# A two-stack fp32 model on one core: one norm's rows left unscaled between the stacks, and the first block's order of work rebuilt

## The reference, cut to what is computed

```python
def rmsnorm(x, g):
    return x * rsqrt(mean(x * x, -1) + EPS) * g

def short_conv_pool_mixer(h, w_in, conv_w, pool_w, pool_scale, w_out):   # first block
    u, gate_c, gate_b, pv = split(h @ w_in)                # 4 x 512 columns
    z = causal_conv3(gate_c * u, conv_w)
    y_a = gate_b * z
    pooled = [running_mean(pv_g, w) - pv_g for g, w in (2, 4, 8, 16)]
    y_b = (pooled @ pool_w) * pool_scale
    return concat(y_a, y_b) @ w_out

# first stack
mem_n = rmsnorm(mem, mem_norm)
h = x
h = h + short_conv_pool_mixer(rmsnorm(h, mix_norm[0]), ...)
h = h + memory_cross_attn(rmsnorm(h, xattn_norm[0]), mem_n, ...)
h = h + peer_ffn(rmsnorm(h, peer_norm[0]), ...)
# second layer: sparse attention + HGRN mixer, cross attention, peer_ffn
h = rmsnorm(h, final_norm)
# second stack, first layer: MLA + dilated attention
hn = rmsnorm(h, attn_norm_2[0])
c_q, c_kv, k_r, qB, kB, vB = split(hn @ e_w_in_2)
qA = rmsnorm(c_q, g_q) @ w_uq                              # ... attention, output projection
h = h + mix                                                # h is the normed one
# swiglu, sliding-window attention, swiglu, rmsnorm
```

## Time and profile before

| | |
|---|---|
| median of 3 runs | 2925.32 us (2921.53 to 2931.91) |
| profiled execution | 2916.09 us |
| its span | 2914.3 us |
| mean granted clock of PE | 0.983 of 2.4 GHz |
| busy: PE / DVE / ACT / POOL | 2777.4 / 1997.9 / 1467.2 / 357.9 us |
| DMA | 546.19 MB, 187 GB/s over the span |

### The profile page before, as it was taken

How to read it: one execution, slowest core, us unless ns; L and a number is a source line. 1 busy time by engine, 2 the same in 40 slices (tenths; PEclk the granted TensorE clock), 3 DMA queues, 4 the chain that set the end, 5 groups by cost and what they waited for, 6 DMA issues and landing times.

```text
span 2914.3 us, 57278 instructions
## 1 busy us (share of the span) xinstructions
PE 2777.4 (95%) x19576; PEld 2604.7 (89%) x19576; DVE 1997.9 (69%) x4331; ACT 1467.2 (50%) x2412; POOL 357.9 (12%) x207
## 2 busy tenths in 40 slices
PE   6899899999999999989999999999999799999998
PEld 6889799999988888878898999988888689999998
DVE  5556964887467667686598788557677676666665
ACT  4445345444455555455544444445555565455544
POOL 0003785000000000000179100000000000000000
PEclk8999999999999999899999999999999899999999
DMA  4434466545676665324355554666666434553454
GB/s 157 174 145 174 163 213 214 178 172 179 223 258 239 240 245 194 136 96 159 117 198 195 184 178 173 202 238 243 236 247 237 160 112 153 183 201 144 174 188 174
DMA packets 140451, 546.19 MB, mean 187 GB/s; under 512 B 15784, under 2 KB 81592, under 8 KB 83616
## 3 DMA queue, kind: packets, MB, share of 16 engines
q1 hardware_dynamic: 63216, 455.38, 43.5%
q10 hardware_dynamic: 73728, 67.14, 7.4%
q0 software_dynamic: 3376, 21.88, 1.9%
HBM read 505.53 MB, written 40.91 MB: 188 GB/s over the span
## 4 chain that ended last, share of the span: by engine, by line
PE 71%; DVE 10%; DMA 7%; POOL 5%; ACT 4%; issue 3%; SPq 0%; ACTq 0%; DVEq 0%
PE bank L779 21%; PE bank L781 20%; PE bank L780 20%; DMA ring<-in_w_stream 6%; POOL wL L542 5%; PE bank L997 4%; DVE wL L542 3%; ACT wH L532 3%; PE bank L900 1%; PE bank L920 1%; PE bank L911 1%; PE bank L796 1%; PE bank L1110 1%; DVE sq L1763 0%; DVE act_out L1750 0%
## 5 line engine op out<-in xcount | busy, mean ns | idle before, releaser
L542 DVE TENSOR_TENSOR wL<-ring,wH 128x1024 fp32r<-128x1024 f32 x742 | 906.3, 1224 | 651.5 <-ACT wH L532 647.6
L532 ACT ACTIVATE wH<-ring 128x1024 fp32r<-128x1024 f32 x864 | 908.2, 1055 | 411.9 <-DMA ring<-in_w_stream 211.6
L779 PE MATMUL bank<-hnH,wH 128*128 128x256 f32 x3528 | 1019.5, 289 | 38.2 <-DVE wL L542 18.1
L780 PE MATMUL bank<-hnL,wH 128*128 128x256 f32 x3528 | 1001.8, 284 | 0.0
L781 PE MATMUL bank<-hnH,wL 128*128 128x256 f32 x3528 | 1001.7, 284 | 0.0
L779 PEld LDWEIGHTS bank<-hnH,wH 128*128 128x128 f32 x3528 | 680.0, 193 | 47.7 <-issue 17.3
L780 PEld LDWEIGHTS bank<-hnL,wH 128*128 128x128 f32 x3528 | 680.6, 193 | 0.8 <-issue 0.5
L781 PEld LDWEIGHTS bank<-hnH,wL 128*128 128x128 f32 x3528 | 679.7, 193 | 0.0
L779 PE MATMUL bank<-wH,wgtH 128*128 128x512 f32 x1024 | 399.1, 390 | 5.1 <-issue 4.5
L780 PE MATMUL bank<-wL,wgtH 128*128 128x512 f32 x1024 | 399.1, 390 | 0.0
L781 PE MATMUL bank<-wH,wgtL 128*128 128x512 f32 x1024 | 399.1, 390 | 0.0
(11 more groups left out here) (399 smaller groups left out, 3572.1 us busy)
## 6 DMA issues: line engine op xcount, KB each, us to landing
ring<-in_w_stream SPq DMA_DIRECT2D x432, 1024.0 KB, 4.9
act_parked<-act_out ACTq DMA_DIRECT2D x256, 128.0 KB, 3.3
act_in<-act_parked ACTq DMA_DIRECT2D x256, 128.0 KB, 2.7
sw_bias<-in_c_swa POOLq DMA_DIRECT2D x1, 4096.0 KB, 14.5
relb_rows<-rel_table POOLq DMA_DIRECT2D x1, 2048.0 KB, 9.6
h_parked<-h POOLq DMA_DIRECT2D x2, 1024.0 KB, 7.3
h_back<-h_parked POOLq DMA_DIRECT2D x2, 1024.0 KB, 6.2
od_relb<-relb_rows POOLq DMA_DIRECT2D x2, 1024.0 KB, 7.5
```

The costliest lines, as they stand in the source:

```text
L532: eng.activation(wH[:, b % NBUF, :], raw(b), ACT.Copy).then_inc(w_high, 1)
L542: eng.tensor_tensor(wL[:, b % NBUF, :], raw(b), wH[:, b % NBUF, :].bitcast(F32), ALU.subtract).then_inc(w_low, 1)
L779: pe.matmul(dst, lh, rh, start=start, stop=False, skip_group_check=True)
L780: pe.matmul(dst, lh, rl, start=False, stop=False, skip_group_check=True)
```

## The change

*First block.* Mix0 is now in RAW with all 16 even_in groups. ACT squares x, then makes highs of x times gain; DVE the lows; the first three blocks' conversions stand behind the first two chunks. Mix0's and mem's squares are gathered. The sum of squares of mem is taken by PE after even_in 2, its squares and root on ACT follow at once; its reciprocal and scaled rows stay with DVE, behind the pooled lows and the first gate. DVE reads all even_in groups, times the root; u is scaled by the root's square (`root2`), so that the product c x u out of the bank needs no scaling, and the gate is scaled by the root before it meets b. PE computes the pool groups between even_in 11 and 12, and even_out begins with the pool's chunks 4 to 7. The Exp of the lower bounds moves behind the square root of mem. The fetch of `mem_raw` and `ev_cnt` waits for the first pair of weights.

*Between the stacks.* Mix2 moves ahead of final and is in RAW with mla_in 0 to 12. Its rows are the unnormed h times the product of both gains (L2052 in the new numbering, made once early); its squares are taken of h times sqrt(g² + EPS), g being final's gain (made once early, too), and its square root has a bias of EPS²: since mean(h² x (g² + EPS)) + EPS² = mean(h² x g²) + EPS x (mean(h²) + EPS), this is the root of both norms at once. DVE reads mla_in times this root, half by half for kB; ACT reads vb times the roots by token (`own_roots`). The sums of final are taken by PE after mla_in 10; `h` is rescaled behind the kB reads.

The core of the diff:

```diff
-GATHERED = [n[0] for n in NORMS if n[0] not in ("mix0", "mem", "x0")]
+GATHERED = [n[0] for n in NORMS if n[0] != "x0"]
+RAW = {"mix0": [("even_in", m) for m in range(16)], ..., "mix2": [("mla_in", m) for m in range(13)], ...
@@ POOL
-            pool.dma_start(mem_raw, mem).then_inc(mem_in, 16)
...
-            pool.dma_start(ev_cnt, c_cnt).then_inc(cnt_in, 16)
+            pool.wait_ge(slot_in[0], 16)
+            pool.dma_start(mem_raw, mem).then_inc(mem_in, 16)
+            pool.dma_start(ev_cnt, c_cnt).then_inc(cnt_in, 16)
@@ PE, first block
-            lin("even_in", range(8), hn, first=lambda k: normed("mix0", k))
+            lin("even_in", range(3), hn, first=lambda k: normed("mix0", k))
             rms("mem")
-            lin("even_in", range(8, 16), hn)
+            lin("even_in", range(3, 12), hn)
             for j in range(4):
...
-            read_of(pe, ("pool", 3))
-            pe.wait_ge(ev_y, 4)
-            lin("even_out", range(8), (ycatH, ycatL))
+            lin("even_in", range(12, 16), hn)
+            lin("even_out", range(8), (ycatH, ycatL), parts=(4, 5, 6, 7, 0, 1, 2, 3),
+                first=lambda k: pe.wait_ge(ev_y, k + 1) if k < 4 else read_of(pe, ("pool", k - 4)))
@@ PE, between the stacks
-            rms("final")
-            rms("mix2")
-            lin("mla_in", range(3), hn, first=lambda k: normed("mix2", k))
+            lin("mla_in", range(3), hn, first=lambda k: normed("mix2", k), norm_of="mix2")
             for m in range(3, 13):
...
+                if m == 10:
+                    rms("final")
@@ ACT, first block
+            act.wait_ge(x_in, 16)
+            for c in range(DC):
+                act.activation(sq[:, c, :], h[:, c, :], ACT.Square).then_inc(sq_done, 1)
+            act.wait_ge(con_in, 32)
+            for c in range(2):
+                raw_high(c)
+            for b in range(LEAD):
+                split_high(act, b)
+            for c in range(2, DC):
+                raw_high(c)
+            root(("norm", "mix0"), D)
+            feed(act, NO[("even_in", 0)])
+            act.wait_ge(mem_in, 16)
+            for c in range(DC):
+                act.activation(sq[:, c, :], mem_raw[:, c, :], ACT.Square).then_inc(sq_done, 1)
...
+            root(("norm", "mem"), D, mem_root)
+            act.wait_ge(lb_max, 1)
+            act.activation(lbv[:, 8:16], lbv[:, 0:8], ACT.Exp).then_inc(lb_exp, 1)
             for m in range(16):
-                dst = ev_pv[:, m, 16:272] if m < 4 else (ev_u, ev_c, ev_b)[(m - 4) % 3][:, (m - 4) // 3, :]
-                copy(("even_in", m), dst)
+                feed(act, NO[("even_in", m)])
@@ ACT, squares(name)
+                if name == "mix2":
+                    act.wait_ge(gains_made, 1)
...
+                    act.activation(sq[:, c, :], h[:, c, :], ACT.Square,
+                                   scale=small[:, 56 + c:57 + c] if name == "mix2" else 1.0).then_inc(sq_done, 1)
@@ ACT, between the stacks
+            squares("mix2")
             squares("final")
-            squares("mix2")
             for m in range(13):
-                    copy(("mla_in", m), ml[m], rows=96 if m in (3, 4) else P)
...
+                feed(act, NO[("mla_in", m)])
...
+                if m == 10:
+                    root(("norm", "final"), D, ml_roots[:, 2, :])
@@ DVE, first block
+            for m in range(4):
+                scaled(("even_in", m), ev_pv[:, m, 16:272]).then_inc(read_by["dve"], 1)
...
+                ps = take(("even_in", 4 + 3 * j))
+                dve.tensor_tensor(ev_u[:, j, :], ps[:, 0:T], root2, ALU.mult).then_inc(read_by["dve"], 1)
+                ps = take(("even_in", 4 + 3 * j + 1))
+                dve.tensor_tensor(ev_cu[:, j, 2:258], ps[:, 0:T], ev_u[:, j, :], ALU.mult).then_inc(read_by["dve"], 1)
@@ DVE, between the stacks
-            rms("final")
             rms("mix2")
+            own(ml_t)
+            for m, dst in enumerate((ml_cq[:, 0, :], ml_cq[:, 1, :], ml_ckv)):
+                scaled(("mla_in", m), dst).then_inc(read_by["dve"], 1)
...
+            for c in range(1, DC - 1):
+                gather("final", c)
...
+            for m in range(9, 13):
+                halves_by_root(("mla_in", m), ml_kB[:, :, m - 9, :])
+            rms("final")
```

More of the change, by code:

```diff
@@ L187, in plan_groups @@
         blocks.append((("even_in", m, 0), ("even_in", m)))
-        if m == 7:
+        if m == 2:
             norm("mem")
-    blocks.append((("pool",), ("pool", 3)))
-    for j in range(4):
-        g(("pool", j), "both")
+        if m == 11:
+            blocks.append((("pool",), ("pool", 3)))
+            for j in range(4):
+                g(("pool", j), "both")
     lin("even_out", 8, "dve")
@@ L262, in plan_groups @@
             g(("ckv2_sq",), "act")
+        if m == 10:
+            norm("final")
     for tt in range(NT):
@@ L826, in lin @@
                 lead = ms[0:LEAD] if first is not None else []
-                summed = bank(("norm", norm_of)) if lead and norm_of and norm_of != "mix1" else None
+                summed = bank(("norm", norm_of)) if lead and norm_of and norm_of not in ("mix1", "mix2") else None
                 held = [bank((name, m)) for m in lead]
@@ L1332, in squares @@
-                if name == "final":
-                    feed(act, NO[("norm", name)] + 1)
+                if name != "final":
+                    root(("norm", name), D, bias=small[:, 92:93] if name == "mix2" else eps)
                 if name in REWRITTEN:
@@ L2056, in _ @@
-            for j in range(4):
-                ps = take(("pool", j))
-                dve.wait_ge(bank_high, both_no[("pool", j)] + 1)
-                dve.scalar_tensor_tensor(ycatL[:, 4 + j, :], ps[:, 0:T], V("even_pool_scale", j),
-                                         ycatH[:, 4 + j, :].bitcast(F32), ALU.mult,
-                                         ALU.subtract).then_inc(read_by["dve"], 1)
+                ps = take(("even_in", 4 + 3 * j))
+                dve.tensor_tensor(ev_u[:, j, :], ps[:, 0:T], root2, ALU.mult).then_inc(read_by["dve"], 1)
```

243 lines of the change are left out of this document (142 added, 101 removed).

## The result

| | before | after |
|---|---|---|
| median | 2926.59 us (2921.53 to 2931.91, 4 runs) | 2894.91 us (2888.05 to 2900.45, 4 runs) |
| ratio | | 0.9892, 95% interval 0.9869 to 0.9914 |
| profiled execution | 2916.09 us, span 2914.3 | 2900.45 us, span 2898.7 |

The median fell by 31.7 us, the profiled executions by 15.6. Both are right, and the first thing to learn here is how. A second set of runs of the changed kernel gave 0.9882 (0.9859 to 0.9904), medians of 2928.23 and 2891.75 us.

A forecast was written before the change was run, and what follows sets the result against it. TensorE, 71% of the span, was taken as the bound, with time won only where it stands still or runs at half clock. Gains of 14.3 + 12.2 = 26.5 us took 2925.3 to 2898.8 us, range 2885 to 2912.

The forecast's parts named there:

- First block: Start to even_out's last read: 13.5 us gained, ending at 104.3 instead of 117.81 us; 12.2 after x0's table load.
- Between the stacks: Copy of the sums to first uq read: gain 14.3 us, lower bound 7.5, upper bound 22.8.
- It becomes 2889.6: Whole kernel: the profiled execution of 2916.09 us becomes 2889.6 after the summed gain of 26.5 us.
- TensorE waits 2.2 us more at b16: Between the stacks: TensorE waits 2.2 us at weight block b16, which DVE converts only after rescaling h.
- DVE becomes the bound: First block: DVE's list grows from 59.36 to 64.2 us, against 46 us of even_in and pool products.
- Plus 1.5 for half clock: End of first block: 1.5 us added to even_out's remaining 21.8 us for half clock, giving 104.3.
- The memory fetch: Start of first block: fetching memory later is free; first weight pair estimated at 10.5 us with 1.5 MB sent later.
- The pool product: First block: pool precedes in the order of even_out's parts, so the 6.4 us wait for ycatL goes.
- The table load at x0: After the first block: ACT loads Sqrt again before x0's squares, costing 1.3 us, all on the path.
- (1): Rival, either stage: DVE's lateness goes round the weight ring; sign, wL waits over 10 us; gain near 15, 2910 us; chance 0.16.
- (2): Rival, both places: TensorE or the shorter list binds if DVE hardly idles; gain 41, 2884 us; chance 0.06.
- (3): Rival, first block and mla_in: clock stays at 0.50, TensorE binds again; +10.4 us, 2936 us; chance 0.04.

The follow-up runs named there:

- e4: Changed kernel with memory's scaled rows, lows, highs and small lower-bound operations moved behind the last gate, under even_out; 2891.55 us, ratio 0.9869 to the kernel before.
- e5: Changed kernel with DVE's rescaling of h moved behind the MLA attention, before the additions after e_out; 2890.18 us, ratio 0.9865 to the kernel before.
- e9: The changed kernel again as it is, for another profile; median 2891.75 us.
- e7: Changed kernel with the pool product back behind even_in 15 and even_out's parts in the order 0 to 7; 2898.84 us, one execution.
- e6: Changed kernel with the transfers of memory rows and ev_cnt back at POOL's start; 2908.17 us, one execution.
- e3: Changed kernel with a small extra square root on ACT before the cross attention, loading the Sqrt table early; 2896.38 us, one execution.
- e10: Changed kernel: memory's rows under even_out with two blocks converted within, Sqrt load before memory's highs, h rescaled late, b19's low before last gate's taps; 2882.28 us, 0.9855.

## Why the prediction was right, point by point

*The sum.* 26.5 us were forecast, the 1.3 for x0 taken off; 27.2 is what the same stages gave (15.0 + 12.5 - 0.3); the median moved by 31.7 (interval 25 to 38). The step that failed is one that I did not give a term: that the profiled execution stands for the rest. "It becomes 2889.6" missed by 10.9 us (2900.45), since the stages without an edit took 11.6 us more (peer0 10.9, second layer 2.9, the rest 2.2 less). For the same reason uq's first read came at 2340.73 us and not "near 2328". The forecast held because it was put on the median: peer0 alone varies by 14 us between executions, so that a forecast for the profiled one could only have come true by luck.

*Between the stacks*, 14.3 forecast, 13.0 at the first read of uq and 12.5 at the end of the stage. The walk held in most rows. First product 3.6 us after the copy: 3.77. Key rotation in front of b8 makes PE wait 2.1 us: 2.31. Rescaling done 54.6 us after the copy: 2331.05 - 2275.43 = 55.6. The missed step is "TensorE waits 2.2 us more at b16": it did not wait there in this execution. Behind the wait for the key rotation the clock fell (0.83 from 30 to 40 us after the copy, and so in nine of the ten profiles of this place), which the walk had not, so that PE was still busy with the wide products of vb. In e4's profile the clock stays at 1.00 there, and PE does wait at b16, 1.25 us; its first product of uq starts 59.75 us after the copy, no sooner than in the changed kernel (59.74). The rescaling cost 2.9 us (e5) and not 5. The end came 1.2 us later than the walk said. The row of e4:

```profile
2324.30 0.50 PE L791 MATMUL bank<-wH,hnH 128*128 128x512 f32 x1 [1.25 <-DVE wL L546]
```

*First block*, 13.5 forecast, 15.0 in the first profile, 13.8 in e9's (to 117.81). "DVE becomes the bound", list 64.2 us: 64.36. Its idling, 8.2 by the walk: 8.1. Last ycatL 82: 81.34. b19 at 81.1: 80.58. "Plus 1.5 for half clock" was not paid in this execution (clock 1.00 at 80 to 95 us), but it was in e5 and e7, whose windows at 80 to 85 us stand at 0.66 and whose blocks end at 104.2, my 104.3. Whether it is paid is chance: the end was right by the mechanism, within 1.5 us either way.

*The memory fetch.* I put it at nothing and the first pair at 10.5 us; the first `wH` starts at 9.4. Its own cost was nothing, but what it gives was not in the sum as such: undoing it puts the third `wL` and the last ycatL 3.9 us later (e6), because every microsecond at the head of DVE's list comes out at its end. The 5.2 us of e6's block hold 1.4 of clock besides.

*The pool product.* "Pool now precedes, so the 6.4 us wait for ycatL goes": the wait went, but this reason was wrong. e7 has the old order and ends where e5 does (104.23, 104.24). In the kernel before PE waited for the last gates on DVE, and with the rows and the fetch early these are early too; no run takes that apart further.

*The table load at x0*, 1.3 forecast: 1.42 us of wait, on the path (e3 ends the stage 1.3 us sooner). The term was mis-sized where the clock falls behind it: 3.0 us in four of seven profiles. The Trainium skill, "ScalarE: Activation LUTs", section "What ACT_TABLE_LOAD costs", adds a drain to each load: no row here shows one, since the load starts 0.02 us behind the read before it, and the next activation 0.01 us behind the load's end.

*The rivals.* (1), DVE's lateness round the ring, has two answers. Between the stacks it did not come: one wait of 2.3 us. In the first block my own sign for it did: "waits for wL of over 10 us" were 13.3 us, in six waits. The sign was badly chosen. If DVE is the bound, as I had it, PE must wait for it about that long, whatever the ring does, and the block ended where the walk had it. (2) adds 6 us where the block's own bound has 8 more; with 8 it would be 2882 us, and it did not come either, DVE idled 8.1 us. (3), the clock, is the one that left traces. The whole stage never fell to 0.50, but behind single waits PE ran for a few microseconds at or near half clock: behind the 4.2 us near 62 us (66 in e6) in all seven profiles that have them (0.50 to 0.65 in the 4 us after), behind 1.8 to 2.9 us in front of even_out's third block in four of eight, behind 2.4 us at x0 in four of seven. The Trainium skill, "TensorE: Matmul & The Clock Gate", section "HAM oscillation — how this bites in real kernels", tells of a kernel whose clock falls in each of its gaps. The traces agree for the wait of 4.2 us, in part for those of 1.8 to 2.9 us, by chance of the execution, and not for the 0.96 us at x0 (1.00 in all six). So "by that rule (3) would be the result" took a rule for long gaps and laid it on short ones.

## What to carry to other kernels

Before work is costed on a full engine, look for the stretch where that engine waits anyway: the rescaling cost nothing behind the attention, and 2.2 to 3.3 us where it stood. Then look at what stands behind the new place: memory's rows held up even_out by 5.5 us, but moved under it they held up the next blocks, and in e4 3.3 were lost again; e10 mended part of it by converting two of these blocks within memory's rows. Write a walk of the engine's new list, instruction by instruction, as here: it gave the end of DVE's list to within 0.7 us in the first block and 1.2 between the stacks, though a wait of PE that it had did not come. Compare profiles stage by stage, between marks, before a difference of two spans is believed. And compare ends of a stage at the same clock: e7's 1.4 us looked like the edit's until e5 was laid beside it.

## What the runs showed that I had not expected

Stages with equal code differed by 14 us (peer0, 904.4 to 918.4) and 18 us (second layer, 1126.5 to 1144.1) between executions, where the edited places scattered by 1 to 3. PE's clock after a wait of 2.4 us was 0.50 for some 3 us in four of seven profiles with the same instructions there, and 1.00 in three; after 0.96 us it was 1.00 in all six. And 1.5 MB of transfers, asked for 8 us later, were worth 3.9 us at the end of a block that DVE bounds.
